# A hybrid decoder trunk: index scores on row halves, front loads on one queue, top-k rounds between index additions, recurrence steps a unit forward

## The reference

```python
h = x * (1.0 + sc1) + sh1
p = h @ w_in[l]
q, k, v, qi, ki, wi, xr, yg = jnp.split(p, split_at, axis=-1)
...
# attention: 4 heads of 128; indexer: 8 heads of 64, one shared index key ki
rel = relu(einsum('bthd,bsd->bths', qi_b, ki))
idx_score = einsum('bths,bth->bts', rel, wi_b)      # causal
_, sel = top_k(idx_score, 128)                      # each query attends to these keys
...
# recurrence (RG-LRU), 512 channels
r, i = sigmoid(block_diagonal(xc) ...), sigmoid(block_diagonal(xc) ...)
log_a = -8 * r * softplus(-lam);  a = exp(log_a)
u = sqrt(-expm1(2 * log_a)) * (i * xf)
h = associative_scan(a, u)
```

## Time and profile before

| | |
|---|---|
| median of 3 runs | 1347.91 us (1347.04 to 1349.14) |
| the profiled execution | 1348.19 us, span 1346.3 us |
| TensorE busy | 1284.8 us (95%), granted clock 0.988 on the mean |
| VectorE busy | 792.2 us (59%) |
| ScalarE busy | 551.9 us (41%) |
| GpSimd busy | 156.7 us (12%) |
| moved by DMA | 158.58 MB, mean 118 GB/s |

### The profile page before, as it was taken

The page is one execution under the profiler, slowest core; times in us unless marked ns, Lnnn a source line. Parts: engine busy times, 40 slices in busy tenths (PEclk is TensorE's granted clock), DMA queues, the critical chain, the costliest instruction groups (busy, mean ns, idle before and its releaser), DMA issues.

```text
span 1346.3 us, 17154 instructions
## 1 busy us (share of the span) xinstructions
PE 1284.8 (95%) x6260; PEld 1016.4 (75%) x6260; DVE 792.2 (59%) x1302; ACT 551.9 (41%) x849; POOL 156.7 (12%) x129
## 2 busy tenths in 40 slices
PE   3999998899999999999999999979999999999996
PEld 1776766678788888888877776757878888888885
DVE  2656989656753734536476489885574343443354
ACT  3743555634632413314347435574273142231331
POOL 3000335001000000000120013520200000000012
PEclk8999999899999999999999999999999999999998
DMA  9753445031343242343245434431123333323311
GB/s 311 252 169 125 145 137 174 31 110 50 109 142 123 93 156 96 106 154 97 78 132 163 138 124 149 149 102 32 63 79 111 100 102 94 93 94 100 103 64 63
DMA packets 73398, 158.58 MB, mean 118 GB/s; under 512 B 6528, under 2 KB 10872, under 8 KB 73336
## 3 DMA queue, kind: packets, MB, share of 16 engines
q1 hardware_dynamic: 59904, 108.61, 25.8%
q0 software_dynamic: 12800, 48.76, 10.8%
q10 hardware_dynamic: 632, 0.39, 0.1%
HBM read 155.64 MB, written 2.10 MB: 117 GB/s over the span
## 4 chain that ended last, share of the span: by engine, by line
PE 82%; ACT 6%; DVE 6%; issue 2%; DMA 2%; POOL 1%; POOLq 0%; ACTq 0%; DVEq 0%; SPq 0%
PE bank L645 24%; PE bank L647 23%; PE bank L646 23%; PE bank L690 2%; DMA first_mod<-in_w_mod_dram 2%; PE bank L610 2%; PE bank L548 1%; ACT resid L1020 1%; PE bank L836 1%; PE bank L850 1%; ACT w_hi L988 1%; DVE resid L1453 1%; PE bank L870 1%; ACT turned_ring L1086 1%; DVE w_lo L1444 1%
## 5 line engine op out<-in xcount | busy, mean ns | idle before, releaser
L1444 DVE TENSOR_TENSOR w_lo<-w_raw,w_hi 128x1024 fp32r<-128x1024 f32 (+1 forms) x192 | 207.7, 1098 | 337.0 <-ACT w_hi L988 337.0
L988 ACT ACTIVATE w_hi<-w_raw 128x1024 fp32r<-128x1024 f32 (+1 forms) x216 | 203.7, 960 | 464.2 <-PE bank L647 462.4
L645 PE MATMUL bank<-a_hi,w_hi 128*128 128x512 f32 x896 | 372.0, 415 | 4.0 <-DVE w_lo L1444 3.1
L646 PE MATMUL bank<-a_lo,w_hi 128*128 128x512 f32 x896 | 350.2, 391 | 0.0
L647 PE MATMUL bank<-a_hi,w_lo 128*128 128x512 f32 x896 | 350.1, 391 | 0.0
L645 PEld LDWEIGHTS bank<-a_hi,w_hi 128*128 128x128 f32 x896 | 168.6, 188 | 56.0 <-issue 16.0
L645 PE MATMUL bank<-b_hi,w_hi 128*128 128x512 f32 x512 | 199.7, 390 | 0.0
L647 PE MATMUL bank<-b_hi,w_lo 128*128 128x512 f32 x512 | 199.2, 389 | 0.0
L646 PE MATMUL bank<-b_lo,w_hi 128*128 128x512 f32 x512 | 199.2, 389 | 0.0
L646 PEld LDWEIGHTS bank<-a_lo,w_hi 128*128 128x128 f32 x896 | 168.8, 188 | 40.2 <-issue 5.8
L647 PEld LDWEIGHTS bank<-a_hi,w_lo 128*128 128x128 f32 x896 | 168.6, 188 | 36.3
(11 more groups left out here) (260 smaller groups left out, 1461.0 us busy)
## 6 DMA issues: line engine op xcount, KB each, us to landing
mod_raw<-in_w_mod_dram POOLq DMA_DIRECT2D x40, 1024.0 KB, 5.9
w_raw<-in_w_up_dram SPq DMA_DIRECT2D x64, 512.0 KB, 3.7
w_raw<-in_w_down_dram SPq DMA_DIRECT2D x64, 512.0 KB, 3.7
w_raw<-in_w_in_dram SPq DMA_DIRECT2D x48, 512.0 KB, 3.9
w_raw<-in_w_out_dram SPq DMA_DIRECT2D x16, 512.0 KB, 3.7
first_mod<-in_w_mod_dram SPq DMA_DIRECT2D x4, 1024.0 KB, 19.9
first_mod<-in_w_mod_dram POOLq DMA_DIRECT2D x4, 1024.0 KB, 15.5
x_in<-in_x_dram POOLq DMA_DIRECT2D x4, 512.0 KB, 15.1
```

The lines of the kernel that those rows point to most:

```text
L645: mm(o, wh, hi(kk), start=first, stop=False)
L646: mm(o, wh, lo(kk), start=False, stop=False)
L988: last = af(hi, src, ACT.Copy)
L1444: last = tt(lo, src, hi.bitcast(F32), ALU.subtract)
```

## The change

- **Index scores.** The rows of a `qi` tile stay in their natural order, head 2m on rows 0 to 63 and head 2m+1 on rows 64 to 127. The key is kept once in each half (`ki_twice`). Two heads are two matmuls over 64 rows each, one behind the other, into banks 5 and 6; both banks are waited for ahead of the first. The rotary swap is now within 64 rows, in four copies of 32 rows a tile. The splits of `qi`'s weights are one instruction instead of four, and two memsets are gone.
- **Front.** SP issues both halves of `first_mod`; POOL only `x`. `b_mod` is turned by itself and early. The other vectors are turned behind the first columns, copied by ScalarE after its stage 0, and the decay constants made after stage 1 (ScalarE) and stage 2 (VectorE). TensorE waits for that copy (`p_act` 2) ahead of group `qi`.
- **Top-k.** Eight rounds stand between the index additions of blocks 2 and 3; all later counts are two or more higher, 47 of 48 rounds lie ahead of the attention stage.
- **Attention stage.** The gate products move into units 0 and 1; inputs, square roots, scans and squares each a unit forward; `late_mod` 13 from unit 3 to ahead of unit 8's scores. On GpSimd the decay squares stand ahead of the last low part (`out0`, pair 3), which waits for all scans.

```diff
@@ -366,16 +365,7 @@
...
-            if name != "qi":
-                return [(raw[:, p, :, :], w_hi[:, p, :, :], w_lo[:, p, :, :])]
-            pieces = []
-            for s in range(2):
-                for head in range(2):
-                    src = raw[:, p, s, :].rearrange("p (m head half d) -> p head m half d", m=4, head=2, half=2)[:, head]
-                    hi, lo = (w[:, p, s, :].rearrange("p (m half head d) -> p head m half d", m=4, head=2, half=2)[:, head]
-                              for w in (w_hi, w_lo))
-                    pieces.append((src, hi, lo))
-            return pieces
+            return [(raw[:, p, :, :], w_hi[:, p, :, :], w_lo[:, p, :, :])]
@@ -403,6 +393,9 @@
...
+                if s == FIRST_STAGES - 1:
+                    sp.wait_ge(mod_used, 2)
+                load_first_mod(sp, s, 1)
@@ -460,11 +453,8 @@
...
-                if s == FIRST_STAGES - 1:
-                    pool.wait_ge(mod_used, 2)
-                load_first_mod(pool, s, 1)
-
-            for s in range(FIRST_STAGES - 1):
+
+            for s in range(FIRST_STAGES):
@@ -505,10 +492,13 @@
...
-                    if n == LATE_PAIRS - 2:
+                    if n == LATE_PAIRS - 3:
...
+                    if n == LATE_PAIRS - 2:
+                        pool.wait_ge(lru_out, l * LT + LT)
+                        low_part(*lows[11])
@@ -551,10 +541,14 @@
...
-            pe.wait_ge(p_in_small, 16 * len(VEC))
-            for l in range(DEPTH):
-                last = turn(banks[0][:, l * P:l * P + NV], stage[0:NV, l, :], ident[0:NV, 0:NV])
-            last.then_inc(p_pe, 1)
+            pe.wait_ge(p_in_b, 16)
+            turn(banks[1][:, 0:6 * DK], stage[0:6 * DK, 0, :], ident[0:6 * DK, 0:6 * DK]).then_inc(p_b, 1)
+
+            def turn_vectors():
+                pe.wait_ge(p_in_small, 16 * (len(VEC) - 1))
+                for l in range(DEPTH):
+                    last = turn(banks[0][:, l * P:l * P + NV], stage[0:NV, l, :], ident[0:NV, 0:NV])
+                last.then_inc(p_pe, 1)
@@ -682,13 +676,15 @@
...
+                pe.wait_ge(rope_done, l * 13 + 5)
...
-                    b = 5 + u % 2
-                    pe.wait_ge(rope_done, l * 13 + 5)
-                    pe.wait_ge(free_s[b], uses_before(b, f"idx{u}", l))
-                    mm(banks[b][:, 0:(i + 1) * P], qi[:, h // 2, i * P:(i + 1) * P],
-                       (ki_b if h % 2 else ki_a)[:, 0:(i + 1) * P], start=True, stop=True).then_inc(full_s[b], 1)
+                    pe.wait_ge(free_s[5 + u % 2], uses_before(5 + u % 2, f"idx{u}", l))
+                for h in heads:
+                    u = IDX.index((i, h))
+                    b, rows = 5 + u % 2, slice(h % 2 * IDX_DH, (h % 2 + 1) * IDX_DH)
+                    mm(banks[b][:, 0:(i + 1) * P], qi[rows, h // 2, i * P:(i + 1) * P],
+                       ki[rows, 0:(i + 1) * P], start=True, stop=True).then_inc(full_s[b], 1)
@@ -777,10 +773,12 @@
...
+                    turn_vectors()
+                    pe.wait_ge(p_act, 2)
...
-                    pe.wait_ge(p_const, 9)
+                    pe.wait_ge(p_const, 7)
@@ -816,12 +814,12 @@
...
-                    **dict(zip((19, 20, 22, 23, 25, 26, 28, 29), (idx_head(1, h) for h in range(IDX_HEADS)))),
+                    **dict(zip((20, 23, 26, 29), (idx_pair(1, j) for j in range(IDX_HEADS // 2)))),
...
-                    **{2 * h + 1: idx_head(2, h) for h in range(IDX_HEADS)},
-                    **{HALF + 2 * h + 1: idx_head(3, h) for h in range(IDX_HEADS)}, HALF: lambda: late_mod(l, 4)})
+                    **{4 * j + 2: idx_pair(2, j) for j in range(IDX_HEADS // 2)},
+                    **{HALF + 4 * j + 2: idx_pair(3, j) for j in range(IDX_HEADS // 2)}, HALF: lambda: late_mod(l, 4)})
@@ -885,10 +883,10 @@
...
+                    if u == 6:
+                        late_mod(l, 13)
...
-                    if u == 3:
-                        late_mod(l, 13)
@@ -1045,6 +1050,10 @@
...
+                        if s == 0:
+                            vectors_out()
+                        if s == 1:
+                            lambdas()
@@ -1077,17 +1086,19 @@
...
-                def rope_tile(name, dst, m, scale=1.0):
+                def rope_tile(name, dst, m, scale=1.0, half=64):
...
-                    af(ring[0:64, r, :], banks[m][64:P, :], ACT.Copy, scale=scale)
-                    af(ring[64:P, r, :], banks[m][0:64, :], ACT.Copy, scale=scale).then_inc(free_s[m], 1)
+                    for at in range(0, P, 2 * half):
+                        af(ring[at:at + half, r, :], banks[m][at + half:at + 2 * half, :], ACT.Copy, scale=scale)
+                        last = af(ring[at + half:at + 2 * half, r, :], banks[m][at:at + half, :], ACT.Copy, scale=scale)
+                    last.then_inc(free_s[m], 1)
...
-                        rope_tile("qi", qi[:, m, :], m)
+                        rope_tile("qi", qi[:, m, :], m, half=IDX_DH // 2)
@@ -1221,14 +1232,14 @@
...
-                    if u == 6:
+                    if u == 5:
...
-                    if 10 <= u < 10 + LT:
-                        m = u - 10
+                    if 9 <= u < 9 + LT:
+                        m = u - 9
@@ -1555,10 +1568,11 @@
...
+                    lambdas()
...
-                    ve.wait_ge(p_const, 9)
+                    ve.wait_ge(p_const, 7)
@@ -1590,10 +1604,8 @@
...
-                tt(ki_a[0:32, :], straight[0:32], swapped[0:32], ALU.add)
-                tt(ki_b[32:64, :], straight[0:32], swapped[0:32], ALU.add)
-                tt(ki_a[64:96, :], straight[32:64], swapped[32:64], ALU.subtract)
-                tt(ki_b[96:P, :], straight[32:64], swapped[32:64], ALU.subtract).then_inc(rope_done, 1)
+                tt(ki[0:64, :], straight[0:64], swapped[0:64], ALU.add)
+                tt(ki[64:P, :], straight[0:64], swapped[0:64], ALU.add).then_inc(rope_done, 1)
@@ -1661,28 +1673,37 @@
                 split_lo("v", l, 2)
                 idx_add(1, range(4, 8))
                 split_lo("v", l, 3)
-                idx_add(2, range(0, 4))
-                split_lo("k", l, 0)
-                idx_add(2, range(4, 8))
+                for j in range(3):
+                    idx_add(2, range(2 * j, 2 * j + 2))
+                    topk(2 * j + 2)
+                    if j == 1:
+                        split_lo("k", l, 0)
+                idx_add(2, range(6, 8))
                 conv(0)
                 split_lo("k", l, 1)
+                idx_add(3, range(0, 2))
                 conv(1)
-                idx_add(3, range(0, 4))
+                idx_add(3, range(2, 4))
+                topk(8)
                 split_lo("k", l, 2)
+                idx_add(3, range(4, 6))
                 conv(2)
-                idx_add(3, range(4, 8))
+                idx_add(3, range(6, 8))
                 conv(3)
                 masks()
                 split_lo("k", l, 3)
-                for p, rounds_ in enumerate((6, 12, 18, 22)):
+                for p, rounds_ in enumerate((13, 17, 21, 25)):
                     ve.sem_inc(lo_turn, 1)
                     topk(rounds_)
 
-                def lru_input(m):
+                def lru_gated(m):
 
                     ve.wait_ge(free_s[5], uses_before(5, f"gi{m}", l) + 1)
                     ve.wait_ge(conv_done, l * LT + (m + 1))
                     step(tt(xc[:, m, :], xc[:, m, :], gi[:, m, :], ALU.mult))
+
+                def lru_input(m):
+
                     ve.wait_ge(lru_exp, l * LT + (m + 1))
                     ve.wait_ge(lru_squared, l * LT + (m + 1))
                     stt(th[:, m, :], lru_a2[:, m, :], 1.0, th[:, m, :], ALU.add, ALU.mult).then_inc(lru_m, 1)
@@ -1703,14 +1724,14 @@
...
-                topk(23)
+                topk(26)
...
-                for p, rounds_ in enumerate((26, 29, 32, 34)):
+                for p, rounds_ in enumerate((29, 32, 34, 36)):
...
-                for p, rounds_ in enumerate((37, 39, 42, 45)):
+                for p, rounds_ in enumerate((39, 42, 45, 47)):
@@ -1733,13 +1754,16 @@
...
-                    topk(min(45 + u + 1, 3 * per))
-                    if 2 <= u < 2 + LT:
-                        lru_input(u - 2)
-                    elif 7 <= u < 7 + LT:
-                        lru_scan(u - 7)
-                    if 12 <= u < 12 + LT - 1:
-                        m = u - 11
+                    topk(3 * per)
+                    if u < 2:
+                        lru_gated(2 * u)
+                        lru_gated(2 * u + 1)
+                    if 1 <= u < 1 + LT:
+                        lru_input(u - 1)
+                    elif 6 <= u < 6 + LT:
+                        lru_scan(u - 6)
+                    if 11 <= u < 11 + LT - 1:
+                        m = u - 10
...
```

90 lines of the change are left out of this document (46 added, 44 removed).

## The result

| | kernel before | changed kernel |
|---|---|---|
| median | 1348.99 us (20 runs, 1346.81 to 1351.64) | 1351.76 us (20 runs, 1349.78 to 1354.44) |
| ratio | 1 | 1.0022 [1.0016, 1.0028] |
| profiled execution | 1348.19 us, span 1346.3, clock 0.988 | 1352.54 us, span 1350.6, clock 0.981 |

The change makes the kernel slower by 0.22%, or 2.8 us. The forecast was 1337.1 us with a range of 1328 to 1347; the time lies 4.8 us above the range, and on the side that had 7%. In the two profiled executions the difference is 4.2 us.

A forecast was written before the change was run, and what follows sets the result against it. TensorE, 82% of the chain of waits, was taken as the bound; -3.0 - 12.6 + 1.8 + 4.5 + 1.5 - 3.0 = -10.8 us from 1348.19 gave 1337.4, as median 1337.1. Own range 1332 to 1342, with rivals 1328 to 1347.

The forecast's parts named there:

- the side that had 7%: Whole kernel: the chance given to a measurement showing the changed kernel slower than the kernel before.
- Index scores, -12.6: Index heads, both layers: two heads over 64 rows each overlap, 15.5 us less 24 pairs x 0.12 surcharge, -12.6 us.
- 0.98 - 4 x 0.215: Index pairs: surcharge of 0.12 us for going in and out, taken from the `w_mod` strips' time.
- Rival 1: Index pairs: passes run in program order, a pair takes three slots instead of four, saving 4.9 us; time 1344.8; 12%.
- Handover, +1.8: From group v to k: k waits for ScalarE's v copies behind the last relus, +0.9 us a layer, +1.8.
- Takeout, +4.5 and +1.5: `qi` takeout, layer 1: twenty ScalarE copies for twelve delay `xr`, +4.5 us; one low-clock stretch after it, +1.5 us.
- bank 3 comes free just as it is wanted: 0: `qi` takeout, layer 0: no residual scaling there, so the added copies cost nothing, 0 us.
- Front, -3.0: Kernel start: reordered loads let stage 1 start near 24.9 us instead of 27.87, -3.0 us.
- the copies take 0.43 together: 24.8: Front: ScalarE's copies of the turned vectors follow residual copies ending at 24.3, so they end at 24.8 us.
- Attention stage, -3.0: Attention stages, both layers: two top-k rounds leave VectorE, 3 us, half counted: -1.5 us a stage, -3.0.
- The clock: Layer 1's `qi` takeout: idle TensorE brings one stretch at the 1.2 GHz level, 3.2 us, half charged: +1.5 us.

## Why the prediction was wrong, step by step

From the forecast's -10.8 us to the +4.2 of the profiled executions are 15.0 us: 6.3 at the pairs, 4.8 in the layer norms, 3.8 in the attention stages, 1.6 at the takeout of layer 0 and 1.5 in the front, less 1.8 at the handover and 1.2 at the takeout of layer 1. The steps that failed are the pair's surcharge, the front's path over ScalarE, the "0" of layer 0's takeout, the attention stage's gain, and the clock, charged in one place only.

- **Index scores, -12.6.** The mechanism was right, the surcharge mis-sized: 0.12 a pair, "0.98 - 4 x 0.215", measured 0.4. The strips' own row held only half of it; the other half is in the matmul behind them, 0.43 instead of 0.23, which I did not read. 24 pairs by 0.28 are 6.7 us, which leaves 5.9 of the 12.6. Measured -6.3 in all with the handover: the four pairs of block 3 give 1.9 us a layer, 4 x 0.46 and little more, with k's start in it.
- **Rival 1** gave 4.9 us for the pairs, nearer to the measured 6.3 than my 12.6, but by the wrong mechanism: that is luck.
- **Handover, +1.8.** Measured 0: k's first matmul has no wait. Each pair is 0.28 us dearer than I had it, which is lead for VectorE and ScalarE; that this is the whole reason was not tested.
- **Takeout, +4.5 and +1.5.** Layer 1 was right in mechanism and place, the wait too large: two waits of 1.36 and 2.04 us (I had two over 2), 3.0 more than the 0.44 before, for 4.5. The twenty copies took their 12.1 us, but ScalarE began them 1.5 us earlier against the strips than before, where I had 0.3; why is open. The other 1.8 go with 3.4 us at the low clock, for the 1.5 that I charged. Layer 0, "bank 3 comes free just as it is wanted: 0", failed: +1.6. It was true of the profile I read, which had the clock low at 54.9 to 58.3 ahead of it; the changed kernel had it high there, came earlier and waited 1.33 us. The sum put this term at nothing without asking what eight more copies do there.
- **Front, -3.0.** The step that failed is "the copies take 0.43 together: 24.8". I kept ScalarE's old end, 24.3, but the gains came at 23.1, from a stage 0 that began its second half at 18.26, where I had 16.6, and the tiles and copies before it take 3.6. Stage 1 began at 27.23, not 24.9; the load would have allowed 26.1. 0.6 us of gain are left; another 0.9 of the -1.5 is put down to the high clock at 55 us. (The DMA share in the earlier trace rows is 1.04 and not 1.05; nothing hangs on it.)
- **Attention stage, -3.0.** The last scan did end earlier, by 1.9 us counted from the strip at the stage's start, and TensorE's scores left the pace of the scans 2.8 us earlier. But then four units of TensorE's own pace were left instead of three. Scores in the chain of waits, before and then in the changed kernel:

```profile
254.85 1.13 PE bank L850 x2
...
257.20 0.95 PE bank L850 x2
...
259.49 0.86 PE bank L850 x2
```

```profile
248.97 1.13 PE bank L848 x2
...
251.33 0.86 PE bank L848 x2
...
253.42 0.86 PE bank L848 x2
...
255.62 0.86 PE bank L848 x2
```

 A unit of that kind is 2.1 us, so about 0.8 remained. From the strip ahead of the stage to the one behind it (220.13 to 266.30 before) the profiles of this study have on the mean 45.3 us in layer 0 and 45.4 in layer 1 with the new order (nine profiles), 45.2 and 44.8 with the old (eight). The means mix orders and clock: in layer 1 every profile with the new order had at least 6.8 us of low clock in the stage and took 44.9 to 45.7, the one with the old order and 6.8 us took 44.4, the four with 3.4 us or none 44.0, the three with 10.2 us 46.0. The gain of 1.5 a stage is not there; the term is 0, or a loss. Moving the scans a unit forward mostly moves a unit from in front of them to behind.
- **The clock.** I charged one stretch, and it cost what I charged. I took the others at nothing, and beside the pairs they are the largest item of the profiles: the layer norms, untouched by the change, cost 1.8 + 1.4 + 1.6 us more. The attention stage of layer 1 took 1.6 more with 6.8 us of low clock where before had none; how much of that is the clock and how much the new order is not shown. In medians the clock is less sure. The two profiled executions lie apart, 0.8 us under the median of the kernel before (clock 0.988, where its runs have 0.985 on the mean) and 0.8 above that of the changed one. Over 78 runs of the kernel before the time falls by 0.32 us for each 0.001 of mean clock (correlation -0.72), and the changed kernel's mean is 0.004 lower, 1.3 us. How much of the medians' 2.8 us the clock holds stays open.

Without the clock the profile's stretches sum to about -4.0 us (front -0.6, takeouts +0.7 and +3.0, pairs -6.3, attention -0.8 and 0), or -2.4 if the 1.6 of the last stage are no clock: a small gain where the forecast, its clock term aside, had 12.3.

## What to carry to other kernels

Read a small product's price from two places, its own piece in the chain and the full matmul behind it. When one edit makes TensorE earlier and another makes ScalarE longer, go through the places where they meet with both in force; here moving eight ScalarE operations was worth 5.5 us, more than the whole index rework by itself (0.9994). A stage that the change does not touch took 1 to 2 us more with the clock low in it, so differences of 0.2% need the untouched stages looked at first.

## What the runs showed of the hardware that I had not expected

- Float32 products over 64 rows in the two halves of the array run fully beside each other: four passes of 384 columns in 0.84 us, the time of two. Going in costs 0.2 us (0.84 for 0.65) and coming out 0.2 (0.43 for 0.23), for one product as for two.
- One layer norm and what follows (from 270.46 to the next strip, 396.13, before) took 125.6 to 125.7 us in six profiles without low clock in it (the run with more filler aside), 126.5 to 126.7 with 3.4 us of it (five profiles) and 127.1 to 127.5 with 6.8 (five): about 0.25 us for each microsecond at 1.2 GHz, not 0.5. That part of the stage waits for other engines would explain it and was not tested.
- With both `w_mod` halves on SyncE's queue its fourth load took 10.4 us to issue, and the median landing was 13.3 us, where it had been 19.9 and 15.5 on two queues. The DMA engines' rate was the same, 316 GB/s in the front for 313, and the two loads of stage 1 still took 19.4 and 21.7 us.
